# A two-block decoder kernel on one core: other places for the DMAs that build weight sums

## The chip, the cores and the metric

The kernel runs on 1 core of one Trainium2 chip. The metric is the device time of one execution in microseconds (us). It is the median of the runs named below. Everything is float32 at the interfaces.

## The reference, cut to what matters

Two transformer blocks are applied to x (512 positions, 1024 columns), one after the other:

```python
def first_block(x, mem, ...):
    x = x + hybrid_mixer(rms_norm(x, norm_mix_g), w_in, ..., w_branch, w_out)
    x = x + memory_cross_attention(rms_norm(x, norm_xa_g), mem, mem_norm_g, wq, wk, wv, wo)
    x = x + swiglu(rms_norm(x, norm_ffn_g), w_gate_ffn, w_up_ffn, w_down_ffn)
    return rms_norm(x, final_g)

def second_block(x, ...):
    x = x + _mixer(_rms(x, norm_mix_g), ...)      # three kinds of heads, then w_out_2
    return x + _conv_glu(_rms(x, norm_ffn_g), w_up, ffn_conv_w, ffn_conv_b, w_down)
```

The mixer of the first block has three branches, each `sigmoid(gate) * (branch @ w_branch[n])`; their sum goes through `w_out` and is added to x. Both feed-forward parts end in a product with a down matrix of 2816 x 1024.

## The kernel before, in words

**Matmuls and their weights.** Activations lie in SBUF with the columns on partitions and the 512 positions along the row. Every float32 operand is split in a high and a low part (float32r), and a product is three matmuls: high x high, high x low, low x high. The weights come as a stream of chunks, `PLAN`, mostly of 128 x 1024 (512 KB; those of the down projections are 384 or 320 KB). SyncE loads a chunk into one of five buffers `raw` (`load`, L2719 to L2742), ScalarE copies its high part to `WH` (three buffers, L1076), VectorE subtracts to get the low part `WL` (L1758), and TensorE multiplies (L470). The load of chunk i waits until chunk i-5 has been split by VectorE (`sp.wait_ge(wl, i - NRAW + 2)`), the split of chunk i until TensorE has used chunk i-3.

**Stages in order.** The mixer: v, q, k and further projections, stick-breaking attention woven in between, then three branches named mix1, mix2, mix0 (12 chunks each); `w_out` (8 chunks); the cross attention: `wk_xa` and `wv_xa` (8 chunks each, and a chunk takes half the usual time, since there are only 256 memory positions), `wq_xa` and `wo_xa` (8 each); then ffn 1 in two phases, `ffn_up1` 0 to 23, 28 chunks of `ffn_down1`, `ffn_up1` 24 to 43, and again 28 of `ffn_down1`; then the second block with ffn 2 in the same form.

**Residual and memory.** The three branches are merged into the SBUF tensor `X` by GpSimd (L2573), which overwrites x. So once the last merge is done and its parts are split into ZH and ZL, SyncE loads mem (L2775, into `qx`) and x itself again in four pairs of columns (L2777). VectorE adds each tile of w_out to it (L1982), in a loop (`project`) that for tile m first splits the weights of tile m+2, then adds tile m to X; tile 3's weights are split right behind the add of tile 0. TensorE's w_out tiles rotate through three PSUM banks.

**Weight sums for the down projections.** The product with a down matrix is done with seven instead of eight half-size products per block, which needs four sums of the four quarter planes of the weights. DMAs build these sums in DRAM, in the tensors `sums` (one set of four per feed-forward, 2816 KB a plane). A sum is a plain copy of a plane into `sums`, then an accumulating DMA that adds another plane:

- plane 0 = wd[2] + wd[3], plane 1 = wd[0] + wd[3]
- plane 2 = plane 0 + wd[0], plane 3 = plane 2 + wd[1]

The copy (`copy_in`, L2744 to L2750) goes through SyncE's queue in four parts of 704 KB, with one weight load after each part. The accumulate (`sum_in`, L2603 to L2606) is one DMA of 352 rows of 8 KB, issued by GpSimd; it waits on the semaphore `xs_out` for all copies up to its own (16 for each part). A copy that starts from another sum waits on `eg_in` for the accumulates that must have landed (`ready`). A load of `ffn_down` that takes a summed plane waits for all four accumulates of its set.

**What sets the order.** Each engine has its program written out by hand (`pool_program`, `sp_program` and so on). In SyncE's, `load_to(name, i, ahead)` issues loads until the one `ahead` chunks behind chunk (name, i), exclusive, and the copies stand between such calls. In GpSimd's, the `sum_in` calls stand between the merges and the additions of squares for the norms (`add_squares`, L2563). GpSimd's instructions and its DMAs start in this order, SyncE's too: a wait holds whatever stands behind it.

Of the kernel before, what the change touches and what calls it, by code (L numbers as in the profile page):

```python
# [42 lines left out]
def plane_slice(ph, mp):  # L43
    n = PAIRS[ph][1] * P
    at = mp * P * n + (4 * P * PAIRS[0][1] * P if ph else 0)
    return slice(at, at + P * n), n
# [119 lines left out]
def drain(g):  # L166
    for _ in g:
        pass
# [21 lines left out]
def program(nc, xT, memT, wst, wd1, wd2, cols, rows, wsp, cmat, cmask, outT):  # L190
    es = ExitStack()
    with es:
# [28 lines left out]
        wd = [wd1, wd2]  # L221
        sums = [nc.dram_tensor(f"sums{n}", [4, PLANE_N], F32, kind="Internal").ap() for n in (1, 2)]
# [200 lines left out]
        def evicted(g, n):  # L423
            w, ph, mp = g // 8, g // 4 % 2, g % 4
            if ph and n in (5, 7):
                return x_add, (16, 32)[w] + 2 * mp + (1 if n == 5 else 2)
            return gb, 24 + 56 * w + (32 + 6 * mp if ph else 8 * mp) + n + (0 if ph and n > 5 else 1)
# [4 lines left out]
        def final(which, m):  # L432
            return evicted(8 * which - 4 + m // 2, 5 if m % 2 else 7)
# [2119 lines left out]
        def pool_program():  # L2553
# [4 lines left out]
            def add_squares(which=0):  # L2558
                j = at["sq"]
                at["sq"] += 1  # L2560
                pool.wait_ge(sqr, j + 1)
                pool.wait_ge(acp, j)
                gp.tensor_tensor(acc[:, which, :], acc[:, which, :], sq[j % 2], ALU.add).then_inc(acp, 1)  # L2563
# [5 lines left out]
            def merge(nth, m):  # L2569
                pool.wait_ge(gb, 8 * nth + m + 1)  # L2570
                if nth == 2:
                    pool.wait_ge(mg, m + 1)
                gp.tensor_tensor(X[:, m, :], X[:, m, :], misc[:, 2 + 2 * (m // 2 % 2) + m % 2, :], ALU.add).then_inc(mg, 1)  # L2573

            def branch(nth):
                for mp in range(4):
                    for _ in range(4):
                        yield
                    for e in range(2):
                        if nth:  # L2580
                            merge(nth, 2 * mp + e)
                        yield
# [20 lines left out]
            def sum_in(which, to, plane, ready):  # L2603
                pool.wait_ge(xs_out, 256 * (which - 1) + ready)
                rows_ = [a.rearrange("(r c) -> r c", c=2048) for a in (sums[which - 1][to], wd[which - 1][plane])]
                gp.dma_start(rows_[0], rows_[1], accum_op=ALU.add, max_dma_last_dim=8192).then_inc(eg_in, 16)  # L2606
# [2 lines left out]
            sum_in(1, 0, 3, 128)  # L2609
            sum_in(1, 1, 3, 128)  # L2610
            drain(branch(2))
            for k in range(7):
                add_squares()
            sum_in(1, 2, 0, 192)
            sum_in(1, 3, 1, 256)
            for k in range(7):
                add_squares()
            sum_in(2, 0, 3, 128)
            sum_in(2, 1, 3, 128)
            sum_in(2, 2, 0, 192)  # L2620
# [98 lines left out]
        def sp_program():  # L2719
            sp = Queue(nc.sync)  # L2720
            at = {"load": 0, "main": 1}

            def load(n=1):
                for _ in range(n):
                    i = at["load"]
                    if i < NCH:
                        at["load"] += 1
                        if i >= NRAW:
                            sp.wait_ge(wl, i - NRAW + 2)
                        name, j = PLAN[i]  # L2730
                        if not name.startswith("ffn_down"):
                            nc.sync.dma_start(raw[:, i % NRAW, :], wst[at["main"]]).then_inc(raw_in[i % NRAW], 16)
                            at["main"] += 1
                            continue
                        ph, mp, prod = DOWN[j]
                        w = int(name[-1]) - 1
                        made, plane = PLANE[prod]
                        if made:
                            sp.wait_ge(eg_in, 64 * (w + 1))
                        part, n = plane_slice(ph, mp)  # L2740
                        src = (sums if made else wd)[w][plane, part].rearrange("(p c) -> p c", c=n)
                        nc.sync.dma_start(raw[:, i % NRAW, 0:n], src).then_inc(raw_in[i % NRAW], 16)  # L2742

            def copy_in(which, to, src, ready=None):  # L2744
                if ready:
                    sp.wait_ge(eg_in, 64 * (which - 1) + ready)
                rows_ = [a.rearrange("(r c) -> r c", c=1024) for a in (sums[which - 1][to], src)]
                for x in range(4):
                    nc.sync.dma_start(rows_[0][176 * x:176 * x + 176], rows_[1][176 * x:176 * x + 176]).then_inc(xs_out, 16)
                    load()  # L2750

            def load_to(name, i, ahead):
                load(PLAN.index((name, i)) + ahead - at["load"])

            nc.sync.dma_start(raw[:, 0, 0:512], wst[0, :, 0:512]).then_inc(lead_in[0], 16)
            nc.sync.dma_start(X[:, 0, :], xT[0]).then_inc(lead_in[1], 16)
            nc.sync.dma_start(raw[:, 0, 512:1024], wst[0, :, 512:1024]).then_inc(raw_in[0], 16)
            nc.sync.dma_start(X[:, 1, :], xT[1]).then_inc(x_in[0], 16)
            at["load"] = 1
            for c in range(1, 4):  # L2760
                nc.sync.dma_start(X[:, 2 * c:2 * c + 2, :], xT[2 * c:2 * c + 2].rearrange("k p t -> p k t")).then_inc(x_in[c], 16)
                load()
            load_to("q", 0, 5)
            nc.sync.dma_start(row3[:, :, :], rows[0:3].partition_broadcast(P)).then_inc(row_in, 16)
            nc.sync.dma_start(wT[:, :, :], wsp).then_inc(row_in, 16)
            nc.sync.dma_start(misc[:, 4:6, :], cmask).then_inc(row_in, 16)

            load_to("zu", 0, 5)
            copy_in(1, 0, wd[0][2])
            copy_in(1, 1, wd[0][0])  # L2770
            load_to("w_out", 0, 6)
            sp.wait_ge(mm_, DONE["mix0", "branch", 7])
            sp.wait_ge(zl_ok, 8)
            sp.wait_ge(mg, 16)
            nc.sync.dma_start(mraw[:, :, :], memT).then_inc(mem_in, 16)  # L2775
            for i in range(4):
                nc.sync.dma_start(X[:, 2 * i:2 * i + 2, :], xT[2 * i:2 * i + 2].rearrange("k p t -> p k t")).then_inc(x_in[i], 16)  # L2777

            load_to("wk_xa", 2, 5)
            copy_in(1, 2, sums[0][0], 32)  # L2780
            load_to("wq_xa", 0, 5)
            copy_in(1, 3, sums[0][2], 48)
            load_to("ffn_up1", 2, 5)
            copy_in(2, 0, wd[1][2])
            copy_in(2, 1, wd[1][0])
            load_to("ffn_up1", 15, 5)
            copy_in(2, 2, sums[1][0], 32)
            load_to("ffn_up1", 26, 5)
            copy_in(2, 3, sums[1][2], 48)
            load_to("gate2", 0, 6)  # L2790
            sp.wait_ge(mm_, DONE["ffn_down1", 55])
            nc.sync.dma_start(row2[:, :, :], rows[3:5].partition_broadcast(P)).then_inc(row_in, 16)
            load_to("av", 1, 5)
            sp.wait_ge(spill, 8)
            nc.sync.dma_start(xs.rearrange("k p t -> p k t"), X[:, :, :]).then_inc(xs_out, 16)

            load_to("w_out2", 0, 6)
            sp.wait_ge(xs_out, 528)
            sp.wait_ge(n_v[0], 4)
            sp.wait_ge(n_v[1], 4)  # L2800
            nc.sync.dma_start(X[:, 4:8, :], xs[4:8].rearrange("k p t -> p k t")).then_inc(xb_in, 16)
            sp.wait_ge(yy_l, 4)
            nc.sync.dma_start(X[:, 0:4, :], xs[0:4].rearrange("k p t -> p k t")).then_inc(xb_in, 16)
            load(NCH)
            for m in FINAL_ORDER[:7]:
                sp.wait_ge(*final(2, m))
                nc.sync.dma_start(outT[m], X[:, m, :]).then_inc(out_in, 16)
            sp.wait_ge(*evicted(15, 6))
            nc.sync.dma_start(outT[6, :, 256:T], X[:, 6, 256:T]).then_inc(out_in, 16)
            sp.wait_ge(*final(2, 6))  # L2810
            nc.sync.dma_start(outT[6, :, 0:256], X[:, 6, 0:256]).then_inc(out_in, 16)
            sp.wait_ge(out_in, 9 * 16)
# [3 lines left out]
        @block.sync  # L2816
        def _(e):
            sp_program()
# [13 lines left out]
        @block.gpsimd  # L2832
        def _(e):
            pool_program()
# [99 lines left out]
```

## Time and profile before

| | us |
|---|---|
| median of 3 runs | 1653.04 (1652.33 to 1654.04) |
| the profiled execution, its own time | 1653.56 |
| its span in the trace | 1651.8 |
| TensorE busy (matmul) | 1628.4 |
| VectorE busy | 1027.7 |
| ScalarE busy | 736.9 |
| GpSimd busy | 148.1 |
| HBM read and written | 222.32 MB and 50.36 MB |

How to read it: the times of the rows further down are counted from the start of the span, and the execution's own time is 1.8 us longer than the span. PE is TensorE, DVE VectorE, ACT ScalarE, POOL GpSimd, SP SyncE; a q behind the name is the engine's queue (SPq: a DMA issued by SyncE). L470 is line 470 of the kernel. A gap in brackets is the idle time just before an instruction, with what ended it. Queue q1 holds the DMAs that SyncE issues, q0 those of GpSimd. The granted clock is a share of TensorE's full 2.4 GHz.

### The profile page before, as it was taken

Reading aid. Unit: us, or ns where it says so; the run is one execution under the profiler, and the core shown is the slowest. Engines: PE = TensorE matmul, PEld = TensorE weight load, DVE = VectorE, ACT = ScalarE, POOL = GpSimd, SP = SyncE. Lnnn points to the kernel's source line nnn. Section 1 sums busy time; section 2 is a strip of 40 time slices with the busy share of each in tenths; the row PEclk is TensorE's granted clock in tenths of the full one; section 3 lists DMA queues with packets and bytes.
Section 4 is the critical chain, followed back from the end, with each engine's and each line's share of the span. In section 5 each row is a group of like instructions: output and inputs, shape, how many; then the busy total and the mean of one; then the engine's idle time right before and its main releaser. Section 6 shows DMA issues by size and latency. Waiting matters only on the chain.

```text
span 1651.8 us, 21354 instructions
## 1 busy us (share of the span) xinstructions
PE 1628.4 (99%) x8524; PEld 1351.2 (82%) x8524; DVE 1027.7 (62%) x1481; ACT 736.9 (45%) x1118; POOL 148.1 (9%) x172
## 2 busy tenths in 40 slices
PE   9999999999999999999999989999999999999999
PEld 7788878888877778889988887877777888898889
DVE  5446754554653455656655686757655688777886
ACT  5343334333553344333423366246685555444453
POOL 0000001221210011000000032212101200000000
PEclk9999999999999999999999999999999999999999
DMA  7253222256479224994682353241213232363235
GB/s 263 95 189 106 88 90 74 92 145 187 166 234 292 86 75 166 245 269 134 206 238 86 100 172 115 94 153 62 77 39 127 77 103 96 107 203 107 97 88 179
DMA packets 61379, 227.94 MB, mean 138 GB/s; under 512 B 6800, under 2 KB 7184, under 8 KB 57632
## 3 DMA queue, kind: packets, MB, share of 16 engines
q1 hardware_dynamic: 57152, 199.26, 35.6%
q0 software_dynamic: 3840, 26.77, 7.6%
q8 instruction: 68, 1.11, 0.3%
q10 hardware_dynamic: 288, 0.54, 0.1%
q14 instruction: 31, 0.25, 0.0%
HBM read 222.32 MB, written 50.36 MB: 165 GB/s over the span
## 4 chain that ended last, share of the span: by engine, by line
PE 92%; DVE 3%; ACT 2%; DMA 1%; issue 1%; SPq 0%; DVEq 0%; ACTq 0%
PE pst L470 91%; DMA raw<-wst 1%; DVE WL L1758 1%; DVE XL L1770 1%; ACT WH L1076 1%; PE pst L957 1%; PE pst L638 1%; DVE X L2103 0%; ACT L1081 0%; DVE qx L2002 0%; ACT misc L1076 0%; PE pst L760 0%; DVE ML L1766 0%; DVE misc L2517 0%; ACT Sx L1076 0%
## 5 line engine op out<-in xcount | busy, mean ns | idle before, releaser
L470 PE MATMUL pst<-XH,WH 128*128 128x512 f32 x1312 | 523.7, 399 | 0.6 <-DVE WL L1758 0.6
L1758 DVE TENSOR_TENSOR WL<-raw,WH 128x1024 fp32r<-128x1024 f32 (+2 forms) x343 | 388.2, 1133 | 218.6 <-ACT WH L1076 217.8
L470 PE MATMUL pst<-XH,WL 128*128 128x512 f32 x1312 | 512.4, 391 | 0.0
L470 PE MATMUL pst<-XL,WH 128*128 128x512 f32 x1312 | 511.9, 390 | 0.0
L1076 ACT ACTIVATE WH<-raw 128x1024 fp32r<-128x1024 f32 (+3 forms) x345 | 331.5, 964 | 323.0 <-PE pst L470 313.4
L470 PEld LDWEIGHTS pst<-XH,WH 128*128 128x128 f32 x1312 | 247.0, 188 | 61.6 <-issue 11.5
L470 PEld LDWEIGHTS pst<-XL,WH 128*128 128x128 f32 x1312 | 247.1, 188 | 52.0 <-issue 2.6
L470 PEld LDWEIGHTS pst<-XH,WL 128*128 128x128 f32 x1312 | 246.8, 188 | 52.1
L470 PE MATMUL pst<-TH,WH 128*128 128x256 f32 x616 | 176.0, 286 | 4.5 <-DVE WL L1758 3.5
L470 PE MATMUL pst<-TL,WH 128*128 128x256 f32 x616 | 175.2, 284 | 0.0
L470 PE MATMUL pst<-TH,WL 128*128 128x256 f32 x616 | 175.1, 284 | 0.0
L470 PEld LDWEIGHTS pst<-TH,WH 128*128 128x128 f32 x616 | 118.9, 193 | 6.4 <-DVE WL L1758 4.3
L1076 ACT ACTIVATE misc<-misc 128x512 f32<-128x512 f32 x86 | 54.3, 631 | 149.7 <-DVE misc L2150 81.5
L470 PEld LDWEIGHTS pst<-TL,WH 128*128 128x128 f32 x616 | 119.0, 193 | 0.2
L470 PEld LDWEIGHTS pst<-TH,WL 128*128 128x128 f32 x616 | 119.0, 193 | 0.0
L470 PE MATMUL pst<-ZH,WH 128*128 128x512 f32 x224 | 89.3, 398 | 0.0
L470 PE MATMUL pst<-ZH,WL 128*128 128x512 f32 x224 | 87.3, 390 | 0.0
L470 PE MATMUL pst<-ZL,WH 128*128 128x512 f32 x224 | 87.3, 390 | 0.0
L2563 POOL TENSOR_TENSOR acc<-acc,misc 128x512 f32<-128x512 f32 x35 | 54.0, 1543 | 301.9 <-ACT misc L1076 300.6
L2517 DVE SCALAR_TENSOR_TENSOR misc<-gp,colsb,misc 128x512 f32<-128x512 f32 x88 | 66.1, 751 | 23.4 <-ACT misc L1076 21.8
L1076 ACT ACTIVATE TH<-misc 128x256 fp32r<-128x256 f32 (+1 forms) x88 | 49.9, 574 | 45.2 <-DVE misc L2524 31.6
L1076 ACT ACTIVATE misc<-gp,colsb 128x512 f32<-128x512 f32 x44 | 35.9, 815 | 58.2 <-DVE gp L2543 58.2
(285 smaller groups left out, 1926.2 us busy)
## 6 DMA issues: line engine op xcount, KB each, us to landing
raw<-wst SPq DMA_DIRECT2D x232, 512.0 KB, 3.4
sums<-wd POOLq DMA_DIRECT2D x8, 2816.0 KB, 20.6
raw<-sums SPq DMA_DIRECT2D x32, 384.0 KB, 3.1
sums<-wd SPq DMA_DIRECT2D x16, 704.0 KB, 5.9
sums<-sums SPq DMA_DIRECT2D x16, 704.0 KB, 7.3
raw<-sums SPq DMA_DIRECT2D x32, 320.0 KB, 3.0
raw<-wd SPq DMA_DIRECT2D x24, 384.0 KB, 3.3
raw<-wd SPq DMA_DIRECT2D x24, 320.0 KB, 2.9
```

Of the source, the lines that this page charges most:

```text
L470: return nc.tensor.matmul(out, lhs, rhs, start=start, stop=stop, skip_group_check=more)
L638: ins = nc.tensor.transpose(ps[b0 + e][:, j * P:(j + 1) * P], sg_[:, s, e, j * P:(j + 1) * P], ident)
L957: ins = nc.tensor.transpose(ps[b0 + e][:, j * P:(j + 1) * P], Sx[:, s, e, j * P:(j + 1) * P], ident)
L1076: return nc.scalar.activation(out, in_, func, **kw)
L1758: vec.tensor_tensor(WL[:, i % NHL, 0:n], raw[:, i % NRAW, 0:n], WH[:, i % NHL, 0:n].bitcast(F32), ALU.subtract).then_inc(wl, 1)
L1770: vec.scalar_tensor_tensor(XL[:, m, :], X[:, m, :], gain, XH[:, m, :].bitcast(F32), ALU.mult, ALU.subtract).then_inc(xl, 1)
L2517: vec.scalar_tensor_tensor(o, gp[:, e, j:T + j], col[:, a:a + 1], o, ALU.mult, ALU.add).then_inc(hs, 1)
L2563: gp.tensor_tensor(acc[:, which, :], acc[:, which, :], sq[j % 2], ALU.add).then_inc(acp, 1)
```

## The change

The accumulate of plane 2 of the first set moves on GpSimd from behind the squares of the first norm to just behind the last merge of the mixer, and that of plane 3 from before the squares of the third norm to behind them. On SyncE the copy of plane 2 moves into the mixer's last branch (mix0), that of plane 3 into the first up projection, in front of the copies of the second set. Those of its planes 0, 1 and 3 come later than before, those of plane 2 slightly earlier. The first copy of the second set gets a wait (`ready=0`: all four accumulates of the first set have landed), and `copy_in` tests for `None` so that 0 counts.

```diff
@@ pool_program
             drain(branch(2))
+            sum_in(1, 2, 0, 192)
             for k in range(7):
                 add_squares()
-            sum_in(1, 2, 0, 192)
-            sum_in(1, 3, 1, 256)
             for k in range(7):
                 add_squares()
+            sum_in(1, 3, 1, 256)
             sum_in(2, 0, 3, 128)
@@ sp_program
             def copy_in(which, to, src, ready=None):
-                if ready:
+                if ready is not None:
                     sp.wait_ge(eg_in, 64 * (which - 1) + ready)
...
             copy_in(1, 1, wd[0][0])
+            load_to("mix0", 9, 5)
+            copy_in(1, 2, sums[0][0], 32)
             load_to("w_out", 0, 6)
...
-            load_to("wk_xa", 2, 5)
-            copy_in(1, 2, sums[0][0], 32)
-            load_to("wq_xa", 0, 5)
+            load_to("ffn_up1", 1, 5)
             copy_in(1, 3, sums[0][2], 48)
-            load_to("ffn_up1", 2, 5)
-            copy_in(2, 0, wd[1][2])
+            load_to("ffn_up1", 12, 5)
+            copy_in(2, 0, wd[1][2], 0)
             copy_in(2, 1, wd[1][0])
-            load_to("ffn_up1", 15, 5)
+            load_to("ffn_up1", 24, 5)
             copy_in(2, 2, sums[1][0], 32)
-            load_to("ffn_up1", 26, 5)
+            load_to("ffn_up1", 35, 5)
             copy_in(2, 3, sums[1][2], 48)
```

The orders of TensorE, VectorE and ScalarE are the same in both kernels. On GpSimd, from the end of the second branch to the start of the second block; `sums<-wd` is an accumulate, `X<-X,misc` a merge, `acc<-acc,misc` an addition of squares:

```order
 L2606 DMA sums<-wd 352x2048 x2
 L2573 TENSOR_TENSOR X<-X,misc 128x512 x8
-L2563 TENSOR_TENSOR acc<-acc,misc 128x512 x7
-L2606 DMA sums<-wd 352x2048 x2
-L2563 TENSOR_TENSOR acc<-acc,misc 128x512 x7
-L2606 DMA sums<-wd 352x2048 x4
+L2606 DMA sums<-wd 352x2048
+L2563 TENSOR_TENSOR acc<-acc,misc 128x512 x14
+L2606 DMA sums<-wd 352x2048 x5
 L2563 TENSOR_TENSOR acc<-acc,misc 128x512 x14
 L2627 MEMSET kz 128x2048
```

The third accumulate now follows the last merge with nothing between them, and the fourth stands behind all 14 additions of squares.

On SyncE, from the copies of planes 0 and 1 to the first of plane 2 (`sums<-sums` is a part of such a copy, `raw<-wst` a weight load):

```order
 L2732 DMA raw<-wst 128x1024
 L2749 DMA sums<-wd 16x11264
-L2732 DMA raw<-wst 128x1024 x46
-L2775 DMA qx<-memT 128x2048
-L2777 DMA X<-xT 128x2x512 x4
-L2732 DMA raw<-wst 128x1024 x9
+L2732 DMA raw<-wst 128x1024 x42
 L2749 DMA sums<-sums 16x11264
 L2732 DMA raw<-wst 128x1024
```

The copy of plane 2 now stands four loads ahead of the reload of mem and x, where it stood nine loads behind it.

Further on in the same queue, behind that copy:

```order
 L2732 DMA raw<-wst 128x1024
 L2749 DMA sums<-sums 16x11264
-L2732 DMA raw<-wst 128x1024 x11
+L2732 DMA raw<-wst 128x1024
+L2777 DMA qx<-memT 128x2048
+L2779 DMA X<-xT 128x2x512 x4
+L2732 DMA raw<-wst 128x1024 x40
 L2749 DMA sums<-sums 16x11264
 L2732 DMA raw<-wst 128x1024
```

The copy of plane 3 comes 40 loads after the reload; the stretch of the cross attention has no copy any more.

## Rows read from the trace of the kernel before

**Rows 1.** The page: span and busy time by engine.

```profile
span 1651.8 us, 21354 instructions
PE 1628.4 (99%) x8524; PEld 1351.2 (82%) x8524; DVE 1027.7 (62%) x1481; ACT 736.9 (45%) x1118; POOL 148.1 (9%) x172
```

**Rows 2.** Timeline of TensorE, two stretches: start, us, instruction [idle before <-releaser].

```profile
468.36 0.50 PE L470 MATMUL pst<-WH,MH 128*128 128x512 f32 x1 [2.80 <-DVE WL L1758]
...
505.23 0.66 PE L710 MATMUL pst<-cm,qx 128*128 128x128 f32 x4 [1.36 <-ACT kx L1076]
```

**Rows 3.** Timeline of ScalarE at the same place.

```profile
502.27 1.06 ACT L1076 ACTIVATE WH<-raw 128x1024 fp32r<-128x1024 f32 x1 [2.23 <-DMA raw<-wst]
```

**Rows 4.** Timeline of GpSimd, its accumulating DMAs and one merge.

```profile
353.13 2.14 POOL L2606 DMA_DIRECT2D sums<-wd  x2
...
416.81 1.80 POOL L2573 TENSOR_TENSOR X<-X,misc 128x512 f32<-128x512 f32 x1 [0.68 <-DVE misc L1845]
...
480.98 0.92 POOL L2606 DMA_DIRECT2D sums<-wd  x1 [14.09 <-DMA sums<-sums]
...
674.90 1.87 POOL L2606 DMA_DIRECT2D sums<-wd  x2 [40.48 <-DMA sums<-wd]
```

**Rows 5.** L2606's DMAs from issue to landing: of 480 to 503, then of 674 to 712.

```profile
DMA to landing us min/median/max: 20.8/20.8/20.8
...
DMA to landing us min/median/max: 19.0/27.6/36.1
```

**Rows 6.** Weight loads (L2732) from issue to landing, those of 356 to 382.

```profile
DMA to landing us min/median/max: 10.7/15.0/17.7
```

**Rows 7.** Timeline of SyncE's queue: the reload of mem and x.

```profile
420.45 0.33 SPq L2775 DMA_DIRECT2D qx<-memT  x1
420.82 2.27 SPq L2777 DMA_DIRECT2D X<-xT  x4
```

**Rows 8.** The first x load (L2777) from issue to landing.

```profile
DMA to landing us min/median/max: 5.8/5.8/5.8
```

**Rows 9.** Timeline of VectorE around that reload.

```profile
426.69 0.69 DVE L1982 TENSOR_TENSOR X<-X,pst 128x512 f32<-128x512 f32 x1 [5.18 <-DMA X<-xT]
427.29 1.22 DVE L1758 TENSOR_TENSOR WL<-raw,WH 128x1024 fp32r<-128x1024 f32 x1
...
432.56 0.69 DVE L1982 TENSOR_TENSOR X<-X,pst 128x512 f32<-128x512 f32 x1 [0.99 <-PE pst L470]
...
437.93 0.69 DVE L1982 TENSOR_TENSOR X<-X,pst 128x512 f32<-128x512 f32 x1 [2.46 <-PE pst L470]
```

**Rows 10.** DMA queues in 360 to 386: packets, MB, share of 16 engines.

```profile
q0 software_dynamic: 557, 4.43, 81.7%
q1 hardware_dynamic: 557, 2.05, 21.1%
```

**Rows 11.** The same in 732.4 to 733.6.

```profile
q0 software_dynamic: 28, 0.23, 93.0%
q1 hardware_dynamic: 30, 0.09, 21.1%
```

**Rows 12.** The same in 421.5 to 424.5 (mem), then in 425 to 430 (x).

```profile
q1 hardware_dynamic: 115, 0.94, 78.9%
...
q1 hardware_dynamic: 1026, 2.00, 105.6%
```

**Rows 13.** Windows of TensorE: busy us (matmuls), granted clock, DMA share, GB/s.

```profile
469.60:473.00 3.40, 3.40 (x9) 0.50 0.95 370
473.10:476.50 3.40, 3.40 (x17) 1.00 1.01 419
```

**Rows 14.** Timeline of SyncE's queue, the last load of the first up phase.

```profile
723.94 0.34 SPq L2732 DMA_DIRECT2D raw<-wst  x1
```

**Rows 15.** Timeline of VectorE in the first down projection.

```profile
767.95 0.96 DVE L1758 TENSOR_TENSOR WL<-raw,WH 128x768 fp32r<-128x768 f32 x1 [1.20 <-ACT WH L1076]
...
770.11 0.96 DVE L1758 TENSOR_TENSOR WL<-raw,WH 128x768 fp32r<-128x768 f32 x1 [0.60 <-ACT WH L1076]
```

## The prediction

> **What bounds the kernel now.** I read the page first: TensorE is busy for 1628.4 of 1651.8 us [rows 1]. So all its idle time together is 23.4 us, and an edit that moves only DMAs can win no more than the part of it that DMAs cause. In TensorE's timeline I then looked for each gap and for who ended it; two lie where the change works. The one of 2.80 us at 468.36 was ended by VectorE's own work, a weight split. The one of 1.36 us at 505.23 was ended by ScalarE's copy of kx [rows 2], and ScalarE was late because it had waited 2.23 us for a weight load just before [rows 3]. That load ran beside the accumulating DMA that GpSimd issued at 480.98 and that took 20.8 us to land [rows 4, 5]. This is the one place where the sums cost TensorE time today.
>
> Then the two queues. While an accumulate runs, the engines carry 557 packets of queue 0 (8 KB each, the accumulate) and 557 of queue 1 (weights) in 26 us, and are busy without a break: 81.7% and 21.1% [rows 10]. So a pair of packets costs 26 x 16 / 557 = 0.75 us, of which the accumulate's is 0.817 x 26 x 16 / 557 = 0.61 us. One accumulate is 2816 KB in 352 packets, 22 for each of 16 engines, and for those 22 turns queue 1 gets one packet a turn whatever its size. Right after the two queues met in a later stage, 1.2 us show 28 and 30 packets on the 16 engines [rows 11]: about two of each, so they do take turns one by one. A weight load (8 packets an engine) then lands in 10.7 to 17.7 us [rows 6], and TensorE has no gap there: a load is issued as soon as the split five chunks before it is done.
>
> **Part 1, the third sum plane.** Its four copies move from 462 to about 390 us, its accumulate from 480.98 to the end of the mixer. On SyncE the copy waits for two landed accumulates; they were issued at 353.13 and together take 36 us (the pair at 674.90 shows 36.1 [rows 4, 5]), so SyncE is held to about 390. Four w_out loads stand behind that wait and between the copies. I cost this at nothing: the cover is the lead of five chunks, which already carries landings of 17.7 us [rows 6] in the same stage; without the cover each copy would cost its own time.
>
> On GpSimd the accumulate now stands right behind the last merge, which ends at 416.81 + 1.80 = 418.6 [rows 4], with its copies landed by about 411. So it starts at 418.6, under 2 us ahead of the reload of mem at 420.45 and of x at 420.82 [rows 7]. Both go through queue 1. Mem has 8 packets an engine (0.789 x 3 x 16 / 115 = 0.33 us each) and each pair of x columns 16 of 2 KB (1.056 x 5 x 16 / 1026 = 0.08 us each) [rows 12]. Alone, the first x pair lands 5.8 us after issue, at 426.6 [rows 8]. Turn by turn with the accumulate, the 22 turns let mem (8) and 14 of x's 16 packets through; the rest follows when the accumulate is done. With the landing time of 20.8 us [rows 5] that is 418.6 + 20.8 = 439.4, and I put the first x pair at **439.5** instead of 426.6.
>
> Who waits: VectorE already stands still for x now, 5.18 us until 426.69. Behind that add in its queue is the weight split of w_out's tile 3, which ends at 427.29 + 1.22 = 428.5, 1.9 us after the landing. TensorE ends tile 2 at 432.5 (it released the add at 432.56) and needs this split next [rows 9]. So today there are 4.0 us to spare. With x at 439.5 the split ends at 441.4, and TensorE stands for 441.4 - 432.5 = **8.9 us**. ScalarE's and VectorE's further steps hang on the same landing. VectorE idles 3.8 us of the 11.2 between its adds at 426.69 and 437.93, so it needs 7.4 us for that stretch; from 439.6 it is through at 447.0, while TensorE's tile 3 (5.4 us, as between the adds at 432.56 and 437.93) ends at 446.8 or later. It catches up within that tile, and everything behind (the norm, the 2.80 us gap) only shifts.
>
> The clock: after the 2.80 us gap the granted clock is at 0.50 for 3.4 us, with 9 matmuls where the next 3.4 us have 17 [rows 13]: 8 x 0.2 = **1.6 us** lost at 1.2 GHz. A stop of 8.9 us will not cost less than one such stretch, I take one; the bounds are none and two (3.2 us).
>
> Gone is the accumulate of 480.98 with its copies: **-1.4 us**, the gap at 505.23. Next late there is nothing: without an accumulate, loads land well before ScalarE needs them. The second accumulate of that stage (523 us) costs TensorE no gap today, so its removal gives 0.
>
> **Part 2, the fourth plane.** Copies at about 623 to 648, accumulate from 655 to 675, in the up projection with 5.4 us a chunk. Nothing: the same stage carries two accumulates in a row at 674.90 without a gap. GpSimd's squares now come before it in its queue and wait for nothing new.
>
> **Part 3, the second set.** The copies of its first two planes go between the last eight loads of the first up phase, so their last one follows the load of 723.94 [rows 14]; it lands at about 730, then both accumulates start and land 36.1 us later [rows 5], near 767. SyncE's new wait (all four sums of set one) is met at 675, before the copy at 685. The danger is the down projection, where a chunk lasts 2.2 us (770.11 - 767.95 [rows 15]). Its sixth chunk is split by VectorE at 770.11, so its load must be in by 769. It is sixth in a row of loads that, at 8 turns of some 0.75 us each, get 6 us apiece until 767 and then go freely; by that count it lands at 767.5. Cost 0, with 1.5 us to spare; if the accumulates end 3 us later, up to 3 us. The third and fourth planes of the set are copied at 819 and 872 and accumulated until about 915, in up chunks of 5.4 us and before the steep part of the second down phase: nothing.
>
> **Sum**, against the profiled execution's own 1653.56 (span 1651.8 and 1.8 around it): 8.9 + 1.6 - 1.4 = +9.1, so 1662.7; that execution lies 0.5 above the median, so **1662.1** on the median's scale. Bounds of the disputed terms: the first x pair between 437.3 (two of x's small packets a turn) and 441, so a stop of 6.7 to 10.4; clock 0 to 3.2; the gain 0 to 1.4; the down stage 0 to 3. This case's own range is 1658 to 1667.
>
> **Rivals.** (A) The queues take turns by larger groups than one packet. Equal counts over 26 us would fit groups of eight, since a weight load has eight; the 1.2 us stretch speaks against it. Then from a first packet at 420.6: eight of the accumulate to 425.5, mem to 428.1, eight to 433.0, x to 434.8 with its completion. The stop is 434.8 + 1.9 - 432.5 = 4.2, the sum +4.4, time 1657.4. The Trainium skill, in DMA: Bandwidth & Descriptors, section on queues, rings and completion order, says the engine drains a whole packet of typically 9 to 17 descriptors from one queue before it switches. By nine this would put x at about 436.0 and the time at 1658.6, an estimate from that page; the 28 and 30 of [rows 11] disagree if the profile's packets are such descriptors.
>
> (B) The other side: x comes in time. The point is a landing of 430.6 (432.5 - 1.9); the accumulate would have to put its first packet after mem's and x's, that is 7 us after its issue, or yield to queue 1. Then only the -1.4 is left: 1651.7, no slower than before. For it: x itself is small (0.08 us a packet) and alone needs only 1.3 us. Against it: in every meeting of the two queues in this trace the weight loads lose 7 us and more.
>
> (C) Part 3's count is too kind: the two accumulates still run when the down loads need a chunk each 2.2 us and get one in 6. Then some 4 us come on top: 1666.
>
> (D) The change would not do what it says if GpSimd's accumulate waited for late copies, beyond the reload: it needs twelve landed copies at 418.6, and they have 8 us to spare. I give it no chance of its own; it is part of B.
>
> **How the numbers follow.** Forecast 0.72, A 0.10, B 0.10, C 0.08. About 0.2% (3.3 us) is what a measurement of this kernel can tell from no change. Slower by more: forecast, C and nearly all of A, 0.87. Within 0.2%: most of B and the rest of A, 0.10. Faster by more would need B and 2 us that I can't name: 0.03. The range 1656 to 1668 holds the forecast's own range, A and C, and leaves B out.
>
> **What the profile will show.** VectorE's add of the first x pair (L1982) should wait some 18 us for DMA X<-xT and start near 439.6; TensorE should have a gap near 9 us ended by VectorE's split L1758, at w_out's tile 3 (about 441.4), and a granted clock of 0.50 beside it. The 1.36 us gap at L710 should be gone. The stretch of the first down phase should show no new gap. I am wrong in the mechanism if the x landing stays under 431, in size if it lies outside 437 to 441, and in the gain if another gap stands where the one at 505 was.

## The result and the profile after

| | before | changed |
|---|---|---|
| median in the first comparison, 10 runs each | 1651.72 us (1649.38 to 1654.04) | 1657.38 us (1655.87 to 1660.69) |
| the profiled execution, its own time | 1653.56 | 1656.23 |
| its span | 1651.8 | 1654.4 |

The ratio is 1.0035, with a 95% interval of 1.0026 to 1.0044 (as all intervals below): slower by 5.7 us. Two further comparisons of the same kernel, told below, gave 1.0055 and 1.0042. Of all runs one, of experiment 9, took 2708.14 us at a mean granted clock of 0.556; its ratio leaves that run out.

The page of the changed kernel, for [rows 1]:

```profile
span 1654.4 us, 21354 instructions
PE 1625.8 (98%) x8524; PEld 1348.5 (82%) x8524; DVE 1027.3 (62%) x1481; ACT 736.8 (45%) x1118; POOL 149.0 (9%) x172
```

TensorE is busy for 2.6 us less than before and its span is 2.6 us longer, so it stands idle for 5.2 us more. TensorE's timeline, to be set against [rows 2] (start, us, instruction, and in brackets the idle time and what ended it):

```profile
440.30 0.77 PE L470 MATMUL pst<-ZH,WH 128*128 128x512 f32 x1 [8.54 <-DVE WL L1758]
...
478.12 0.50 PE L470 MATMUL pst<-WH,MH 128*128 128x512 f32 x1 [1.61 <-DVE WL L1758]
```

There is a new stop of 8.54 us, ended by VectorE's split of a weight chunk. The gap of 2.80 us in [rows 2] answers to the one of 1.61 us here. The gap of 1.36 us at L710 is gone.

What holds the split up is found by going back along the chain. Here is GpSimd's timeline, for [rows 4], then SyncE's queue, for [rows 7]. In this kernel the mem load is L2777 and the x loads are L2779:

```profile
416.14 1.80 POOL L2573 TENSOR_TENSOR X<-X,misc 128x512 f32<-128x512 f32 x1 [0.68 <-DVE misc L1845]
417.88 0.93 POOL L2606 DMA_DIRECT2D sums<-wd  x1
```

```profile
419.78 0.33 SPq L2777 DMA_DIRECT2D qx<-memT  x1
420.15 2.35 SPq L2779 DMA_DIRECT2D X<-xT  x4
```

The last merge starts 0.67 us earlier than in the trace of before, so all times here compare with that offset. Issue to landing of the accumulate, of mem, and of the four x loads, in this order, for [rows 5, 8]:

```profile
DMA to landing us min/median/max: 19.7/19.7/19.7
...
DMA to landing us min/median/max: 12.9/12.9/12.9
...
DMA to landing us min/median/max: 18.2/19.3/20.5
```

The first x load takes 18.2 us where it took 5.8 [rows 8]. VectorE's timeline, for [rows 9]:

```profile
438.33 0.69 DVE L1982 TENSOR_TENSOR X<-X,pst 128x512 f32<-128x512 f32 x1 [17.50 <-DMA X<-xT]
438.94 1.22 DVE L1758 TENSOR_TENSOR WL<-raw,WH 128x1024 fp32r<-128x1024 f32 x1
```

VectorE waits 17.50 us for x, where it waited 5.18, and the split of w_out's tile 3 stands behind that add. TensorE starts again at 440.30, when the split ends.

The DMA queues (packets, MB, share of 16 engines), for [rows 10, 11]. From 419 to 423.6, with mem issued at 419.78, only one queue moves anything:

```profile
q0 software_dynamic: 96, 0.79, 93.4%
```

So six packets of the accumulate on each of the 16 engines start before the first one of mem. Then 12 us of the overlap, 424 to 436:

```profile
q0 software_dynamic: 232, 1.90, 75.9%
q1 hardware_dynamic: 233, 1.21, 26.0%
```

The counts are equal within one packet, 232 and 233, although the packets of queue 1 are smaller on average (mem's have 8 KB, x's 2 KB): each engine takes one packet of either queue in turn.

The clock, for [rows 13]: windows of TensorE with busy time (matmuls), granted clock, DMA share, GB/s. The first lies in the stop, the second and third behind it, the last behind the second gap:

```profile
436.20:440.20 4.00, 0.00 (x0) 0.50 0.98 368
440.30:446.30 6.00, 6.00 (x14) 0.50 1.03 404
446.50:449.90 3.40, 3.40 (x17) 1.00 0.47 165
478.20:481.60 3.40, 3.40 (x15) 1.00 0.71 205
```

The granted clock falls to 0.50 (1.2 GHz) while TensorE stands still and stays there for 6 us after it has resumed: 14 matmuls in 6 us, where 3.4 us at full clock hold 17. Behind the second gap there is no half clock, while [rows 13] had 3.4 us of it there.

The first down phase of ffn 1, for [rows 15]: the two accumulates of the second set, their landings, and the landings of five weight loads of that stage (L2742) that run beside them:

```profile
735.97 1.88 POOL L2606 DMA_DIRECT2D sums<-wd  x2 [74.36 <-DMA sums<-wd]
...
DMA to landing us min/median/max: 19.8/27.5/35.2
...
DMA to landing us min/median/max: 6.4/10.9/13.3
```

The loads take up to 13.3 us, and TensorE has no new gap there. All four planes of the second set come later than before. For plane 2 the section on the change says "slightly earlier", which is wrong: its first copy is issued at 826.06 instead of 711.66.

So the time can be followed along TensorE's timeline, by the start of the same instructions in both traces. Up to 418 us the changed kernel is 0.67 ahead. There is a small gap in ffn 1, before and in the changed kernel:

```profile
647.96 0.47 PE L470 MATMUL pst<-XH,WH 128*128 128x512 f32 x1 [0.25 <-DVE WL L1758]
...
654.62 0.47 PE L470 MATMUL pst<-XH,WH 128*128 128x512 f32 x1 [0.25 <-DVE WL L1758]
```

The changed kernel is 6.66 behind there: the change has cost 7.3 us in between. The sum of the rows is 8.54 (stop) + 3.0 (6 us at half clock) - 1.19 (2.80 to 1.61) - 1.7 (3.4 us of half clock fewer) - 1.36 (the gap at L710) = 7.3. It is 6.70 behind at 980.20, where the second down phase ends. Then 4.1 us come back in the second block, where the change moves nothing. There the gaps are equal in both traces, and the clock behind them is not. The window behind a gap of 1.9 us, before:

```profile
1244.50:1247.80 3.30, 3.27 (x7) 0.50 0.02 9
```

And the same place in the changed kernel:

```profile
1248.80:1252.10 3.30, 3.30 (x14) 1.00 0.01 3
```

7 matmuls against 14, behind the same gap. Of the twelve traces of this document two have a half clock at this place, that of before and that of experiment 2; what decides it is not shown. Runs of one kernel differ in their mean granted clock too, and the time follows it. Of 63 runs of the kernel before beside the experiments, the 8 at 0.995 have a mean of 1655.0 us, the 24 at 0.996 of 1653.1, the 9 at 0.998 of 1650.4. So one pair of traces must not be read to the microsecond over its whole span, and I compare stretches.

### The profile page after: what moved, and what is told of

The parts are those of the page before. It is cut to its first block, busy times and chain, and to the rows that moved or that the text cites. A ratio compares the mean times of both kernels' runs of the same rounds, so it can differ in the third digit from the quotient of the medians.

```text
span 1654.4 us, 21354 instructions
## 1 busy us (share of the span) xinstructions
PE 1625.8 (98%) x8524; PEld 1348.5 (82%) x8524; DVE 1027.3 (62%) x1481; ACT 736.8 (45%) x1118; POOL 149.0 (9%) x172
## 4 chain that ended last, share of the span: by engine, by line
PE 93%; DVE 3%; ACT 1%; issue 1%; DMA 1%; SPq 0%; DVEq 0%; ACTq 0%
PE pst L470 91%; DMA X<-xT 1%; DVE WL L1758 1%; PE pst L957 1%; DVE XL L1770 1%; PE pst L638 1%; DVE X L2103 0%; ACT WH L1076 0%; ACT L1081 0%; DVE qx L2002 0%; ACT misc L1076 0%; DVE ZL L1766 0%; PE pst L760 0%; DVE ML L1766 0%; DVE misc L2517 0%
## 5 line engine op out<-in xcount | busy, mean ns | idle before, releaser
L2563 POOL TENSOR_TENSOR acc<-acc,misc 128x512 f32<-128x512 f32 x35 | 54.7, 1562 | 314.8 <-ACT misc L1076 313.5
```

## The experiments

The first four shared their runs of the kernel before (24, median 1652.88), the next three theirs (22, 1652.75), and the last three theirs (17, 1652.17). "Changed" is the changed kernel; the diffs are against it unless said otherwise.

**1. The accumulate waits for x.**

```diff
             drain(branch(2))
+            for i in range(4):
+                pool.wait_ge(x_in[i], 32)
             sum_in(1, 2, 0, 192)
```

> The changed kernel with one wait more: GpSimd holds the third accumulate until the four x loads have landed (x_in at 32). Theory (the accumulate and the reload of x take turns on the DMA engines, x comes late and holds VectorE, whose split holds TensorE): the first x pair lands 6 us after its issue again, the 8.5 us gap at w_out's tile 3 goes, and so does the half clock beside it; with the 1.36 us gap at 505 gone as well the time is 1 to 2 us below the kernel before, 0.999. Rival (the copies or the second set, parts 2 and 3, carry the loss): the gap may go, but the time stays 3 us or more above the kernel before, 1.002 or more.

Measured: 1647.85 us, ratio 0.9975 (0.9964 to 0.9986). The first x pair lands 5.9 us after its issue. The stop at tile 3 is gone, and so is the gap at L710. GpSimd's timeline and TensorE's:

```profile
431.46 0.92 POOL L2606 DMA_DIRECT2D sums<-wd  x1 [12.78 <-DMA X<-xT]
...
467.34 0.50 PE L470 MATMUL pst<-WH,MH 128*128 128x512 f32 x1 [1.70 <-DVE WL L1758]
```

So the stop comes from the accumulate beside the reload and from nothing else in the change. This kernel is faster than both, and by 5 us instead of the 1 to 2 expected, so by more than the gap of 1.36 us; experiment 9 comes back to that.

**2. The stop filled with matmuls.** 36 products into a PSUM bank that nobody reads, in front of tile 3; all of the computation stays.

```diff
                 for m in ms:
+                    if name == "w_out" and m == 3:
+                        free(7)
+                        for _ in range(36):
+                            mm(ps[7][:, :], ZH[:, 7, 0:P], ZH[:, 7, :])
```

> The changed kernel with 36 matmuls more on TensorE in front of w_out's tile 3, on a spare PSUM bank, whose result nobody reads; they fill 8.2 of the 8.5 us of the stop. Theory (the stop costs its 8.5 us and then some 2.9 us more because the granted clock stays at 0.50 for 6 us after it): the granted clock stays at 1.00 over the stop, tile 3 starts no later, and the time is 1.5 to 3 us below that of the changed kernel, so 1.0017 to 1.0025 against the kernel before. Rival (the clock's part is nothing, VectorE's chain sets the pace behind the stop): same time as the changed kernel, 1.0035.

Measured: 1657.77 us, ratio 1.0037 (1.0023 to 1.0052). The windows of TensorE in the former stop and behind it:

```profile
436.00:440.60 4.60, 4.60 (x21) 1.00 1.00 336
441.20:447.20 6.00, 6.00 (x27) 1.00 1.04 405
```

The clock stays at 1.00, and 6 us hold 27 matmuls where the changed kernel has 14. Tile 3 starts at 441.11, as late as in experiment 4 (440.98), and at the small gap in ffn 1 this execution is 2.2 us ahead of that one (655.75 against 657.98), although its second gap is 0.6 longer (3.31 against 2.71). So the half clock behind the stop costs 2.8 us by the traces, and by the means of the runs 2.7 (1658.3 against 1661.0). The runs alone would not show it: the intervals of this kernel and of experiment 4 overlap, the ratio lies above the 1.0017 to 1.0025 expected, and it is no lower than the 1.0035 of the first comparison. The 27 matmuls against 14 do show it.

**3. Parts 2 and 3 alone.** Plane 2 of the first set as before, copies and accumulate.

```diff
-            sum_in(1, 2, 0, 192)
             for k in range(7):
                 add_squares()
+            sum_in(1, 2, 0, 192)
...
-            load_to("mix0", 9, 5)
-            copy_in(1, 2, sums[0][0], 32)
...
+            load_to("wk_xa", 2, 5)
+            copy_in(1, 2, sums[0][0], 32)
             load_to("ffn_up1", 1, 5)
```

> Only parts 2 and 3 of the change: plane 2 of the first set copied and accumulated where it was before (behind load wk_xa 6 and behind the first seven squares), plane 3 and the second set as changed. Theory (the whole loss is part 1's): no gap at w_out's tile 3, the gap of about 1.4 us near 505 is back, the down phase has no new gap; time within 1 us of the kernel before, 1.000. Rival (parts 2 and 3 carry a loss, by loads that run beside the two accumulates before the down phase): 1.001 or more with a new gap between 760 and 790.

Measured: 1653.1 us, ratio 1.0005 (0.9995 to 1.0014): nothing. TensorE's timeline in this kernel at the two gaps of [rows 2]:

```profile
467.30 0.50 PE L470 MATMUL pst<-WH,MH 128*128 128x512 f32 x1 [1.70 <-DVE WL L1758]
...
503.80 0.55 PE L710 MATMUL pst<-cm,qx 128*128 128x128 f32 x3 [2.62 <-ACT kx L1076]
```

The first gap is 1.10 us shorter than in [rows 2], the second 1.26 longer, and their sum is the same within 0.2 (4.32 against 4.16). Without its gap TensorE would have come to L710 at 501.18 here (503.80 - 2.62) and at 503.87 in the kernel before (505.23 - 1.36). So it was 2.69 us sooner, and the longer gap, behind weights that the accumulate delays, took 1.26 of them back. The gap at L710 isn't a fixed 1.36: it takes back about half of what is won ahead of it.

**4. The changed kernel again.**

> The changed kernel unaltered, timed beside the other three on the same chip. Its ten runs so far gave 1.0035; I expect 1.0030 to 1.0045, with the gap of 8.5 us at w_out's tile 3. How far its runs differ by the granted clock alone (means of 0.993 to 0.996 so far, 1660.7 to 1655.9 us) is the second thing looked for: if the time follows the mean clock, one thousandth of it is worth about 1.65 us.

Measured: 1661.07 us (6 runs), ratio 1.0055 (1.0041 to 1.0068), above the 1.0030 to 1.0045 expected. TensorE's timeline and its windows behind both gaps:

```profile
440.98 0.76 PE L470 MATMUL pst<-ZH,WH 128*128 128x512 f32 x1 [8.52 <-DVE WL L1758]
...
479.90 0.50 PE L470 MATMUL pst<-WH,MH 128*128 128x512 f32 x1 [2.71 <-DVE WL L1758]
```

```profile
441.00:447.00 6.00, 6.00 (x14) 0.50 1.04 408
481.20:484.60 3.40, 3.40 (x10) 0.50 0.93 302
```

The stop is the same, 8.52. Here the second gap has its old length of 2.71 with a half clock behind it, and at the gap of 0.25 in ffn 1 this execution is 10.0 us behind the kernel before (657.98 against 647.96). That is 8.52 + 3.0 - 0.1 - 1.4.

**5. The third accumulate in rows of 4 KB.** Twice as many packets of half the size.

```diff
-            def sum_in(which, to, plane, ready):
+            def sum_in(which, to, plane, ready, c=2048):
...
-            sum_in(1, 2, 0, 192)
+            sum_in(1, 2, 0, 192, 1024)
```

(c replaces the row length of 2048 in the rearranged tensors and in the largest row.)

> The changed kernel, but the third accumulate goes in rows of 4 KB instead of 8 KB: twice as many packets, each about half as long. Theory (the two queues take turns packet by packet, so what x must wait is 24 packets of the accumulate, whatever their size): 8 turns of 0.31 + 0.33 us for mem and 16 of 0.31 + 0.08 for x put the first x pair at about 434 instead of 438.3, so 14 to 15 us after its issue instead of 18.2, and the stop at w_out's tile 3 falls from 8.5 to about 4.5 us. Rival (the accumulate holds the other queue back until it is done, or shares by time or bytes): x still lands with the accumulate's end, 18 us after its issue, and the stop stays at 8 us or more.

Measured: 1656.4 us, ratio 1.0029 (1.0017 to 1.004), which the changed kernel's first 1.0035 can't be told from; the trace decides. The stop is 6.81 us, less than the 8.52 to 8.64 of the changed kernel, but not the 4.5 expected. Queues in 424 to 428 in this kernel, and then in the changed one:

```profile
q0 software_dynamic: 109, 0.45, 56.7%
q1 hardware_dynamic: 91, 0.75, 46.7%
```

```profile
q0 software_dynamic: 69, 0.57, 67.7%
q1 hardware_dynamic: 67, 0.55, 33.9%
```

In the same 4 us queue 1 gets 91 packets instead of 67, because a turn of the other queue is shorter: 0.567 x 64 / 109 = 0.33 us instead of 0.677 x 64 / 69 = 0.63. Mem lands 10.1 us after its issue instead of 12.9, and the first x pair 16.5 instead of 18.2. That is 3.4 us before the end of the accumulate, which itself takes 22.1 us. So x does not wait for the accumulate's end. The gain is smaller than I expected, since the turns begin late: mem's first packet comes 3.6 us after its issue here and 3.9 us in the changed kernel, in the kernel before 0.95 (421.40 against 420.45).

**6. The first x pair ahead of mem in SyncE's queue.**

```diff
-            nc.sync.dma_start(mraw[:, :, :], memT).then_inc(mem_in, 16)
-            for i in range(4):
+            nc.sync.dma_start(X[:, 0:2, :], ...).then_inc(x_in[0], 16)
+            nc.sync.dma_start(mraw[:, :, :], memT).then_inc(mem_in, 16)
+            for i in range(1, 4):
```

> The changed kernel with the first x pair issued ahead of mem. Theory (turns of one packet): its 16 packets need 16 turns of 0.61 + 0.08 = 0.69 us, 11 us, and it lands some 14.5 us after its issue, near 434.3 on the changed kernel's clock; the stop falls to about 4.5 us; mem lands a little behind the end of the accumulate, near 439. Rival (turns of eight or more packets): the 16 small packets pass in one or two turns, and x lands within 10 us of its issue, with a stop of 1 us or none.

Measured: 1656.56 us, ratio 1.0023 (1.0014 to 1.0033), stop 6.25 us, where I expected 14.5 us for x and a stop of 4.5. X still takes 16.3 us although nothing stands before it; 3.5 of them pass before its first packet. Queues in 424 to 428, where x's packets set in, and in 426 to 430, with packets of 2 KB in queue 1:

```profile
q0 software_dynamic: 90, 0.74, 89.0%
q1 hardware_dynamic: 74, 0.15, 11.4%
...
q0 software_dynamic: 92, 0.75, 90.3%
q1 hardware_dynamic: 90, 0.18, 13.8%
```

Once both run it is 92 packets against 90, with 0.75 and 0.18 MB. Between x's first and last of 256 packets lie 274 of the accumulate. So a packet of 2 KB waits out one of 8 KB, over the whole transfer. Turns in larger groups would have let x's 16 packets an engine through in one or two groups, within 10 us. The Trainium skill, DMA: Bandwidth & Descriptors, in its part on arbitration, says an engine drains a packet of about 9 to 17 descriptors from a queue before it switches. With the profile's packets as descriptors the runs disagree: the turn is one.

**7. Early copy, accumulate behind the squares.** The copies stay in mix0.

```diff
-            sum_in(1, 2, 0, 192)
             for k in range(7):
                 add_squares()
+            sum_in(1, 2, 0, 192)
```

> The changed kernel with the third accumulate back behind the first seven squares (issued near 466), its copy still in the mixer. Theory (early copies cost nothing, the accumulate's place is all): no stop at w_out's tile 3; the accumulate runs from 466 to 487 in the stage where a chunk is used every 2.7 us, so a gap of 0 to 3 us between 480 and 505 stands in the place of the one of 505; the time is that of the kernel before within 2 us, 0.999 to 1.001. Rival (the early copies, or SyncE's wait for the first two accumulates, carry a loss): 1.002 or more, with a gap between 390 and 432.

Measured: 1652.93 us, ratio 1.0002 (0.9993 to 1.0011). There is no stop at tile 3, and none in mix0, so the moved copies cost nothing. But TensorE has a new gap in place of the one at L710, a little over the 0 to 3 us expected:

```profile
488.15 0.50 PE L470 MATMUL pst<-WH,MH 128*128 128x512 f32 x1 [3.78 <-DVE WL L1758]
```

The accumulate, issued at 465.57 into the stage of `wk_xa` and `wv_xa`, makes weight loads land after 9.5 to 17.5 us there. The split that ends the gap stands behind a ScalarE copy that waited 5.78 us for such a load. In that stage a chunk lasts half the usual time, and a load can't be that late.

**8. The changed kernel, a third time.**

> The changed kernel again. Theory (the x transfer lands at about 438 us and stops TensorE for 8.5 us before w_out's tile 3, with a half-clock stretch of 10.2 us there, net 5.7 to 8.7 us by the two comparisons so far): ratio 1.0035 to 1.0055, 1658.5 to 1662 us against 1652.75, so +5.8 to +9.1; the stop in the chain of TensorE is 8.3 to 8.8 us again. Rival (the first comparison was the true size and the second an accident of when the clock falls): +4.5 to +5.5 us. My own forecast of +9.1 lies at the upper end and is right only if the mean of all runs of this kernel is above +8.

Measured: 1659.57 us (5 runs), ratio 1.0042 (1.0029 to 1.0055). The stop is 8.64, the second gap 1.61. At the small gap in ffn 1 it stands 6.9 us behind the kernel before. All 21 runs of the three comparisons have a median of 1658.8 us, against 1652.7 of the 63 of the kernel before beside the experiments: +6.1. That is above the rival's 4.5 to 5.5, though this comparison's interval (+4.8 to +9.1 us) alone does not exclude it. My own +9.1 is too high as the mean size.

**9. The accumulate that waits for x, again** (the kernel of experiment 1).

> The changed kernel with the third accumulate issued only when x has landed, again. Theory (no stop at tile 3, no gap at 503 to 505, and the squares no longer behind a transfer): 0.997 to 0.998 of the kernel before, 1647.8 to 1649.5 us, that is 3.5 to 5 us faster. Rival (the first result was the clock's luck, and only the vanished gap of 1.4 us is real): 1651 to 1652 us, ratio 0.999.

Measured: 1647.7 us, ratio 0.9975 (0.9965 to 0.9986). The best version of the changed kernel stands confirmed. At the small gap in ffn 1 it is at 643.60 against 647.96 before, 4.4 us ahead: 2.80 + 1.36 - 1.70 = 2.5 from the gaps, and 1.7 from a half clock that didn't come. Of this, 1.1 + 1.7 is not the wait's doing: experiment 3 has the short gap and no half clock at the same place too. Against the trace of experiment 3 (646.53) this one is 2.9 ahead, nearly all of it the gap at L710 (2.62). Why the medians of experiments 1 and 9 lie as much as 4.5 to 5 us below the kernel before was not settled.

**10. Part 1 alone, waiting for x.** Against the kernel before:

```diff
             drain(branch(2))
+            for i in range(4):
+                pool.wait_ge(x_in[i], 32)
+            sum_in(1, 2, 0, 192)
             for k in range(7):
                 add_squares()
-            sum_in(1, 2, 0, 192)
             sum_in(1, 3, 1, 256)
...
+            load_to("mix0", 9, 5)
+            copy_in(1, 2, sums[0][0], 32)
...
-            load_to("wk_xa", 2, 5)
-            copy_in(1, 2, sums[0][0], 32)
```

> The kernel before with the third plane's copies and accumulate of the mixer's last branch alone moved, and issued only when x has landed; everything in the down phase as before. Theory (the other two parts cost and bring nothing): within 1 us of the run with all three parts and the wait, about 1648 to 1650 us. Rival (the earlier fourth plane in the first up projection brings part of the gain): 1651 us or more, that is at least 2 us behind that run.

Measured: 1647.38 us (5 runs), ratio 0.9966 (0.9954 to 0.9977). It is within 0.5 us of experiments 1 and 9, so parts 2 and 3 bring nothing here either.

## Why the prediction was right, and where it was off

The forecast was 1662.1 us, +9.1; measured were 1657.38 in the first comparison and a median of 1658.8 over three. The direction, the mechanism and the place are as forecast; the size came out two thirds of it. That it came so near in the traces (+7.0, +7.3 and +10.0) is in part luck, since errors of opposite sign met in the sum.

- **The x landing and the stop**: forecast a landing at 439.5 and a stop of 8.9. The landing came at 438.3, which is 439.0 with the offset of 0.67, and the stop was 8.54, 8.52 and 8.64 in three traces. The way to it was half right. Packets do alternate one by one (experiments 5 and 6). But the forecast shared out all 22 turns of the accumulate. The reload's first packet came 3.9 us after its issue, a wait I had no row for, and six of the turns were gone by then. The 16 left are enough for mem (8) and about half of the first x pair instead of 14 of its 16 packets. Still x landed 0.8 us behind the accumulate, as the rest passed quickly after it. This loss cancelled against the accumulate landing in 19.7 us instead of 20.8.
- **The clock**: forecast one stretch, 1.6 us, bounds 0 to 3.2. Measured 3.0 by the time at half clock and 2.7 to 2.8 by experiment 2. I had priced an 8.9 us stop by what followed one of 2.8. That is a mis-sized term, by 1.1 to 1.4, inside its bounds.
- **"The 2.80 us gap only shifts"**: this is the step that failed. It was 1.61 in two traces of the changed kernel and 2.71 in the third. It isn't the change that sets its length (last section): experiments 1, 3, 9 and 10, where x is in time as before, have 1.70, so the 2.80 of [rows 2] is the exception among them. Where it is short, a half clock behind it is missing too, so 2.9 us hang on it.
- **The gain at L710**: forecast -1.4. The gap is gone in all traces of the changed kernel, and experiments 1, 9 and 10 have none either. The term is right for one pair of traces. But experiment 3 shows that it would have been 2.6 with the shorter gap before it.
- **The copies in mix0, part 2 and part 3**: forecast 0. Experiment 7 shows it for the copies, experiment 3 for parts 2 and 3, and 10 against 1 and 9 once more. In the down phase the last copy was issued at 731.01 and the accumulates ran from 736 to 771.7, some 5 to 7 us behind the forecast, as TensorE itself was (6.7). The sixth down load landed at 772.35, where I had 767.5, which is 774.2 with that delay. Nothing waited, so C did not occur.
- **The sum** of the early terms by the rows: +7.3 and +7.0 where the second gap is short, +10.0 where it is long, around the 9.1 forecast. Over the runs +6.1 is left. Some 4 us of the first trace's come back in the second block through the half clock behind equal gaps (13.6 us of it in three stretches behind 970 us before, 3.4 us in one stretch in the changed kernel). In the trace of before that part has as much half clock as in that of experiment 2 and more than in any other; why the mean over all runs stays 1 to 4 us below the local cost was not settled, since only one execution of each comparison has a trace.
- **The rivals**: A gave 1657.4, nearest to the first median, and yet is not the cause. Its mechanism would have made a stop of 4.2, and the stop is 8.5; experiment 6 is against it too. B (x in time) was wrong: x missed 430.6 by 8 us. It was the right picture of another kernel, though. With x really first, experiment 1 gains not 1.4 but some 5 us.

## What to carry to other kernels

A large DMA that costs nothing beside a steady stream can cost a stop beside a short transfer with a near deadline: look at who reads what is loaded next, count the turns of both queues, and give the large one a wait for the small one. Such a wait cost GpSimd's squares nothing here and turned +6 us into -5. The gap that an edit removes may be larger than its row: if it is ended by a transfer with a fixed end, it swallows part of every gain made ahead of it (1.26 of 2.69 us here).

## What the runs showed of the hardware that I had not expected

**Two engines exclude each other, and either may win.** VectorE's L1770 and GpSimd's addition of squares L2563 start some 30 ns apart at one place where X is split behind the w_out stage. In experiment 4:

```profile
473.22 1.87 DVE L1770 SCALAR_TENSOR_TENSOR XL<-X,colsb,XH 128x512 fp32r<-128x512 f32 x1
...
473.25 1.29 POOL L2563 TENSOR_TENSOR acc<-acc,misc 128x512 f32<-128x512 f32 x1 [3.63 <-ACT misc L1076]
```

In the changed kernel's first trace:

```profile
472.54 0.75 DVE L1770 SCALAR_TENSOR_TENSOR XL<-X,colsb,XH 128x512 fp32r<-128x512 f32 x1
...
472.57 1.87 POOL L2563 TENSOR_TENSOR acc<-acc,misc 128x512 f32<-128x512 f32 x1 [3.63 <-ACT misc L1076]
```

Either VectorE takes 1.87 us and GpSimd 1.29, or VectorE 0.75 and GpSimd 1.87. In the first case the second gap of TensorE is 2.71, 2.80 or 3.31 us (experiment 4, before, experiment 2), in the second 1.6 to 1.7 (the nine other traces). The difference of VectorE's two durations is 1.12 us, that of the gaps 1.10. The Trainium skill, SBUF — State Buffer, in its section on the two separate sides, says that the port pair shared by VectorE and GpSimd is an exclusive lock for the whole instruction, and the loser fully blocks. The rows agree: 0.75 becomes 1.87 on VectorE, or 1.29 becomes 1.87 on GpSimd, and never both. The page also gives the pair to the instruction that starts first. The rows don't show that, since VectorE starts first in both cases, by 33 and 37 ns; what decides is open. Equal code gives both outcomes, and with them come or go 1.1 us of one gap and the 1.7 us of half clock behind it.

**A transfer issued beside a running accumulate starts late.** The reload's first packet came 3.9 us after its issue instead of 0.95. In all six traces in which the reload is issued under 2 us behind the accumulate it is 3.5 to 4.0 us, in the six others 0.95 to 0.96. Only then do the turns begin. What the time goes into is not shown.

**The half clock outlasts the stop.** It held for 6 us after TensorE had resumed behind 8.5 us of idle time, and for 3.4 us behind the gaps of 2.71, 2.80 and 3.31 at the second place. A gap of 1.6 or 1.7 at that place had none in any of nine traces. Length isn't all, though: the gap of 1.9 us at 1244 had 3.4 us of half clock behind it in the trace of before.
